# The sum B12 plus B22 of three up-projection groups, made by GpSimd in place of VectorE

## The reference, cut to what matters

```python
h2 = rms_norm(x, g_ffn)
return x + jnp.square(jax.nn.relu(h2 @ w_up)) @ w_down      # w_up 1024 x 4096, w_down 4096 x 1024
```

## Time and profile before

| | |
|---|---|
| median of 3 runs | 984.46 us (984.36 to 988.92) |
| the profiled execution's own time | 982.63 us |
| its span | 980.7 us |
| VectorE busy | 675.8 us, 69% of the span |
| GpSimd busy | 30.4 us |
| up projection, group 4 to group 6 | 402.87 to 485.40 us of the span |

### The profile page before, as it was taken

The page is one execution under the profiler, slowest core; times in us unless marked ns, Lnnn a source line. Parts: engine busy times, 40 slices in busy tenths (PEclk is TensorE's granted clock), DMA queues, the critical chain, the costliest instruction groups (busy, mean ns, idle before and its releaser), DMA issues.

```text
span 980.7 us, 12406 instructions
## 1 busy us (share of the span) xinstructions
PE 959.9 (98%) x4996; PEld 589.6 (60%) x4996; DVE 675.8 (69%) x1232; ACT 219.1 (22%) x432; POOL 30.4 (3%) x40
## 2 busy tenths in 40 slices
PE   6999999999999999999999999999999999899998
PEld 4944445664555448999844459447854444469543
DVE  5675951235577877975899853788966967675666
ACT  4313321213332133322200011101011321334200
POOL 3000000000000700000000000000000000000000
PEclk9999999999999999999999999999999999999999
DMA  9451731335236524444445434424233434231631
GB/s 317 155 193 42 280 128 43 135 123 172 87 98 192 151 99 172 172 172 143 163 181 181 179 121 151 173 87 172 87 128 130 171 125 145 91 112 45 207 136 43
DMA packets 54424, 139.74 MB, mean 142 GB/s; under 512 B 2864, under 2 KB 6208, under 8 KB 54368
## 3 DMA queue, kind: packets, MB, share of 16 engines
q1 hardware_dynamic: 52448, 134.56, 39.2%
q0 software_dynamic: 1712, 4.32, 1.9%
q10 hardware_dynamic: 208, 0.08, 0.0%
HBM read 137.90 MB, written 1.05 MB: 142 GB/s over the span
## 4 chain that ended last, share of the span: by engine, by line
PE 87%; DVE 7%; DMA 3%; ACT 2%; issue 1%; SPq 0%; DVEq 0%; ACTq 0%
PE pair L1855 40%; PE pair L1936 15%; PE pair L1940 11%; PE pair L2173 6%; DVE arena L904 4%; PE turned L1800 3%; DMA ring<-in_w_in 3%; PE score L2173 3%; PE turned L2173 1%; PE score L2268 1%; PE score L2021 1%; PE score L2330 1%; PE score L2070 1%; PE score L2020 1%; PE score L2343 1%
## 5 line engine op out<-in xcount | busy, mean ns | idle before, releaser
L1855 PE MATMUL pair<-ring,hT 128*128 128x512 f32 (+2 forms) x704 | 298.7, 579 | 0.0
L1855 PEld LDWEIGHTS pair<-ring,hT 128*128 128x128 f32 x704 | 131.7, 191 | 143.6 <-issue 139.8
L904 DVE TENSOR_TENSOR arena<-arena 128x256 f32<-128x256 f32 (+7 forms) x324 | 199.7, 631 | 13.2 <-PE score L2173 4.1
L1855 PE MATMUL pair<-hT,ring 128*128 128x128 f32 (+2 forms) x464 | 76.4, 324 | 0.2 <-ACT hT L587 0.2
L1855 PEld LDWEIGHTS pair<-hT,ring 128*128 128x128 f32 (+1 forms) x464 | 66.0, 188 | 9.0 <-issue 1.3
L904 DVE TENSOR_TENSOR arena<-ring 128x2048 f32<-128x2048 f32 (+1 forms) x35 | 63.1, 1804 | 9.4 <-DMA ring<-in_w_in 5.7
L904 DVE TENSOR_TENSOR arena<-pair,arena 128x512 f32<-128x512 f32 x51 | 35.3, 691 | 48.9 <-PE pair L1940 26.8
L1159 DVE CUSTOM_DVE_ANT_0 arena<-score,masks 128x256 f32<-128x256 f32 (+2 forms) x40 | 18.0, 451 | 71.0 <-PE score L2021 46.6
L1936 PE MATMUL pair<-arena 128*128 128x128 f32 x544 | 64.0, 276 | 0.0
L558 ACT ACTIVATE arena<-turned 128x512 f32<-128x512 f32 (+2 forms) x66 | 32.7, 536 | 136.3 <-PE turned L1800 136.3
L1855 PE MATMUL pair<-ring,arena 128*128 128x512 f32 (+1 forms) x160 | 63.0, 550 | 0.0
(11 more groups left out here) (216 smaller groups left out, 962.7 us busy)
## 6 DMA issues: line engine op xcount, KB each, us to landing
ring<-in_w_in SPq DMA_DIRECT2D x33, 2048.0 KB, 8.4
ring<-in_w_up SPq DMA_DIRECT2D x8, 2048.0 KB, 8.7
ring<-in_w_down SPq DMA_DIRECT2D x8, 2048.0 KB, 7.9
ring<-in_w_o SPq DMA_DIRECT2D x4, 2048.0 KB, 8.0
ring<-in_w_mem_kv SPq DMA_DIRECT2D x2, 2048.0 KB, 7.8
ring<-in_w_glu SPq DMA_DIRECT2D x2, 2048.0 KB, 7.9
ring<-in_w_ssm_out SPq DMA_DIRECT2D x2, 2048.0 KB, 8.5
ring<-in_w_ukv SPq DMA_DIRECT2D x4, 512.0 KB, 3.6
```

The lines of the kernel that those rows point to most:

```text
L904: return dve.tensor_tensor(o, a, b, op)
L1855: ins = pe.matmul(o_, s, m, start=a, stop=b)
```

## The change

GpSimd gets T3 of groups 4, 5 and 6 (`BY_POOL`) as three tensor_tensor instructions behind all that it did before. Each waits for T1 of its group (by `group_sums`) and for the y weights. The sum is written in place onto B12 in the ring, so T3 no longer uses `up_t3` in these groups and no longer waits for Q7 of the group before. VectorE leaves the three instructions out; T2 takes over the wait for the y weights. TensorE's Q7 waits for a new semaphore, `pool_sums`. The counts of `group_sums` are adjusted in a helper `sums_at`.

```diff
+BY_POOL = range(UP + 1, UP + 4)
+def sums_at(i, n):
+    left_out = sum(j in BY_POOL for j in range(i)) + (i in BY_POOL and n > 2)
+    return 4 * i + n - left_out
...
+                if i in BY_POOL:
+                    t3 = b12
...
+            for i in BY_POOL:
+                _, _, (_, b12, _, b22), _, _ = group(i)
+                n = STREAMED.index(JOB[f"g{i}y"])
+                pool.wait_ge(sem("group_sums"), sums_at(i, 1))
+                pool.wait_ge(sem(f"weights{n % RING}"), 16 * (n // RING + 1))
+                pool.tensor_tensor(b12, b12, b22, ALU.add).then_inc(sem("pool_sums"), 1)
...
             def group_t2(i):
                 _, _, (_, _, _, b22), _, (t2, _) = group(i)
+                weights_in(f"g{i}y")
                 dve.wait_ge(sem("group_product"), product_at(i, 5))
...
             for i in range(UP, UP + 4):
-                if i > UP:
-                    group_t3(i)
                 group_t2(i)
...
                 def summed(n):
-                    pe.wait_ge(sem("group_sums"), 4 * i + n)
+                    if n == 2 and i in BY_POOL:
+                        pe.wait_ge(sem("pool_sums"), i - BY_POOL[0] + 1)
+                    else:
+                        pe.wait_ge(sem("group_sums"), sums_at(i, n))
```

More of the change, by code:

```diff
@@ L172 @@
     "group_product": "TensorE: products of the groups of seven, in order", "group_act": "ScalarE: Q1 and Q5 copied, first block out",
-    "group_rows": "sums of a group's rows", "group_sums": "sums of a group's weights: T1, T3, T2, T4",
+    "group_rows": "sums of a group's rows", "group_sums": "sums of a group's weights: T1, T3, T2, T4; T3 is left out where GpSimd makes it",
+    "pool_sums": "GpSimd: T3 of three groups",
     "second_out": "blocks made of sums alone", "group_z": "Q5 less Q7 out of PSUM", "first_out": "Q6 and the second block out of PSUM", "last_out": "the third block out of PSUM",
```

## The result

The changed kernel took 988.01 us (median of 20 runs) against 984.87 us of the kernel before (20 runs beside them): 1.0029 of before, with a 95% interval of 1.0021 to 1.0037, so 2.9 us longer (2.1 to 3.6); the two medians are 3.1 us apart, and the text goes by the ratio. The forecast was 2.0 us, and no change beyond 0.5%.

What follows compares the result with a forecast made beforehand. TensorE, busy 98% of the span, was taken as the bound. Freed VectorE time 0, plus 2.0 us of waiting in group 4, added to 984.46 us gave 986.5 us, range 984.0 to 989.2.

Steps and rivals of the forecast that it cites:

- freed VectorE time is worth 0: Groups 4 to 6: VectorE loses three sums, 6.9 us in all, hidden behind PE, so worth 0.
- The GpSimd sum takes 4.2 us: Each moved T3 sum on GpSimd: 4.2 us, the middle of 3.5 and 4.9, with 6.3 as outer end.
- It starts at T1's end and is in time for Q7: Sums start at T1's end in groups 4 to 6; covers before Q7 are 10.3, 7.1 and 5.3 us, cost 0.
- GpSimd and VectorE take turns by whole instructions: A GpSimd instruction reading SBUF and a two-SBUF-input VectorE one exclude each other; the first to issue holds for its length.
- c_times_f(1) is 3.5 us late against 1.4 us of cover: Group 4, ahead of B's transposes: 2.1 us lost, less about 0.1 of a ScalarE wait, 2.0 us.
- Groups 5 and 6 cost nothing, T4 of group 6 just in time: Groups 5 and 6: squared_turn held, cost 0; T4 of group 6 ends 481.25, Q4 wants it at 481.82, cover 0.6 us.
- a 2 us gap shouldn't lower: Later stages: the granted clock stays up after a 2 us PE gap, since PE already idles 20.8 us of the span.
- Rival A: Groups 4 to 6: VectorE runs on beside GpSimd or GpSimd begins late; cost 0 to 0.3 us, 984.5; chance 0.13.
- rival C: Faster: freed VectorE time would end a wait of TensorE somewhere; no mechanism known; chance 0.03.
- Rival B: Same lock, GpSimd sum near 6.3 us: c_times_f 5.6 late, group 6's T4 misses Q4 by 1.5; 990, +5.6; chance 0.10.

Runs made afterwards that it cites:

- two halves: The changed kernel with each GpSimd sum as two instructions of 128 x 1024, one behind the other; 1.0036 of before (1.0025 to 1.0047).
- two sums: The changed kernel with a second GpSimd sum, B22 + B22 into the unused T3 buffer, ahead of group 4's T3; 1.0069 of before.
- Memsets: The changed kernel with each of GpSimd's three sums replaced by two memsets of 128 x 2048, T3 left out; 0.9997 of before.
- the repeat: The changed kernel run again as it is, against the kernel before; 987.93 us, 1.0017 of before (0.9998 to 1.0037).

## Why the prediction was right, and where it was off

- **TensorE waits for nothing of VectorE's in groups 4 to 6, so freed VectorE time is worth 0.** Right. Groups 5 and 6 kept their length to 0.01 us.
- **The GpSimd sum takes 4.2 us, between 3.5 and 4.9.** Measured 4.52 to 4.54. The bounds held. The middle was 0.3 us low, and every tenth here goes into the loss one to one. The Trainium skill (GPSIMD Engine Reference, "Performance versus the Vector engine") gives 4.497 us for this sum; the three in the trace lie 0.02 to 0.04 us above it.
- **It starts at T1's end and is in time for Q7.** Right: 0.08 us after T1, and no wait of PE for it.
- **GpSimd and VectorE take turns by whole instructions.** Right, and by two separate runs: two halves let exactly one VectorE operation in between, and so did two sums. Memsets, which read nothing, stop nothing. The Trainium skill (SBUF — State Buffer, "Who interferes with whom") says that a GpSimd instruction which only writes SBUF is not in the way of a VectorE instruction with two SBUF inputs; the memsets agree, with 2.36 us for VectorE's two operations beside them.
- **c_times_f(1) is 3.5 us late against 1.4 us of cover.** Measured 3.7 late: 8.24 us from group_last's start to its end where it was 4.53. The transposes waited 2.21 us, and Q2 came 2.34 us later than in step. Forecast 2.0. Of the 0.34 us between them the longer sum is 0.33. The rest nearly cancels: c_times_f(1) ended 3.67 us after GpSimd and not 3.8, the transposes began 0.09 us behind it and not at once, and the first wait for ScalarE gave 0.05 and not 0.1.
- **Groups 5 and 6 cost nothing, T4 of group 6 just in time.** Right; 0.4 us of cover are left of the 0.6 forecast.
- **That "a 2 us gap shouldn't lower" the clock.** This step was wrong. I argued from the clock row of the page, which read 9 in all slices. That row can't show it: a slice is 24.5 us long, and the row reads 9 in all slices of the changed kernel too, whose clock was at 0.50 from 856 to 858. The kernel before had no drop in its trace, but most of its unprofiled runs read 0.998. Behind the new wait the clock fell in one of the two traces of the changed kernel, at a cost of 0.9 to 1.0 us, and 19 of its 30 runs are at 0.997 or below. By these, 2.3 and some 0.6 for the drop is 2.9 us, an estimate; measured 2.9, and 1.7 in the repeat. The intervals of both hold 2.3 as well, so the wait alone would pass too.

Rival A (nothing is held up) and rival C fell with the first trace. Rival B needed a sum of 6.0 us and had one of 4.5.

Putting GpSimd's sum behind c_times_f(1) takes the loss away but gives no gain over the kernel before, since there was none to be had: TensorE never waited for T3.

## What to carry to other kernels

Before work moves from VectorE to GpSimd, look not only at the cover of the moved result but at the VectorE instructions with both inputs in SBUF that will run beside it, and at the semaphores behind them. In this case the delay was GpSimd's whole duration less the time to the next such instruction, within 0.15 us, and the cost was that less the cover of whatever waits. If TensorE waits for nothing of VectorE's, as here, the move has nothing to gain. Where it is wanted for another reason, the sum belongs behind the last instruction whose result is due soon. A trace in which the clock never drops doesn't show that a gap is free, and the page's clock row didn't show one of 3.4 us. Stretches of 2 us and the mean clock of the unprofiled runs did.

## What the runs showed of the hardware beside this

- GpSimd's float32 sum of 128 x 2048 took 4.52 us with two different inputs, written onto one of them, and 3.59 us with the same tensor as both inputs, written to another tile (one instance). Which of the two makes it shorter isn't shown.
- A 128 x 32 operation of VectorE (0.2 us) took 3.90 us when it met the sum: a short instruction is held as a long one is.
- VectorE's 128 x 512 operation with one input in PSUM took 0.69 us beside GpSimd's sum, as long as without it; those with both inputs in SBUF were held.
- With the same waits, one drop of the clock to 0.50 for about 3.5 us happens in most executions, with or without the change. Ten of the twelve traces show it, each behind one of two waits of PE that all these kernels have (1.5 us long near 123, in three traces, or 2.0 us long near 854, in seven). Of 35 runs of the kernel before in one sample, 24 read 0.998 (median 985.11 us) and 11 read 1.0 (982.92). What decides in which executions it comes stays open.
